# FFN up projection: high and low activation halves in one 512-column matmul, two partial sums added on VectorE

## What is computed

```python
def dwconv3(z, w, b=None):
    zp = jnp.pad(z, ((0, 0), (1, 1), (0, 0)))
    y = zp[:, :-2] * w[0] + zp[:, 1:-1] * w[1] + zp[:, 2:] * w[2]
    return y if b is None else y + b

def conv_ffn(h, w_up, conv_w, conv_b, w_down):
    gate, up = jnp.split(dwconv3(h @ w_up, conv_w, conv_b), 2, axis=-1)
    return (jax.nn.silu(gate) * up) @ w_down
```

## Time and profile before

| | us |
|---|---|
| median of three runs (2726.76 to 2734.9) | 2727.99 |
| the profiled execution, its own time | 2725.87 |
| its span, first to last instruction | 2724.2 |
| TensorE busy in the span | 2587.2 (95%) |
| VectorE / ScalarE / GpSimd busy | 1747.4 / 1118.2 / 262.9 |
| mean granted TensorE clock | 0.973 of full speed |

### The profile page before, as it was taken

One profiled execution on the slowest core, in us unless ns is written; L12 is line 12 of the kernel. 1 busy time (PEld: TensorE's weight loads), 2 busy tenths in 40 slices (PEclk: granted clock), 3 DMA queues, 4 the chain that ended last, 5 costly groups with the idle time before them and its releaser, 6 DMA issues.

```text
span 2724.2 us, 44977 instructions
## 1 busy us (share of the span) xinstructions
PE 2587.2 (95%) x16773; PEld 2350.9 (86%) x16773; DVE 1747.4 (64%) x2134; ACT 1118.2 (41%) x1377; POOL 262.9 (10%) x246
## 2 busy tenths in 40 slices
PE   4999989799999999996999999998899999999998
PEld 4989877798998988985888888886699989998997
DVE  4455455678777877667566666665556665666666
ACT  3444343443443443445233333333444434443443
POOL 2100004000000000003000000000011100110110
PEclk9999999899999999997999999998999999999999
DMA  6743369578777777872666655652545565556555
GB/s 160 240 124 95 116 191 273 197 240 277 230 246 254 252 240 244 259 241 85 212 192 191 186 183 184 189 175 96 164 129 181 184 206 172 183 179 207 174 172 172
DMA packets 277979, 523.94 MB, mean 192 GB/s; under 512 B 30696, under 2 KB 100896, under 8 KB 277088
## 3 DMA queue, kind: packets, MB, share of 16 engines
q1 hardware_dynamic: 251616, 403.66, 46.5%
q0 software_dynamic: 25536, 118.29, 14.5%
q10 hardware_dynamic: 704, 0.29, 0.0%
HBM read 511.68 MB, written 10.49 MB: 192 GB/s over the span
## 4 chain that ended last, share of the span: by engine, by line
PE 47%; DVE 3%; ACT 1%; POOL 1%; issue 1%; DMA 0%; POOLq 0%; ACTq 0%; DVEq 0%; SPq 0%
PE ps L1501 17%; PE ps L1509 11%; PE ps L1849 6%; PE ps L1860 5%; PE ps L1854 3%; PE ps L1817 1%; PE ps L1796 1%; POOL alo L533 1%; PE ps L1825 1%; DVE acc L1222 1%; DVE wlo L961 1%; PE ps L1805 1%; ACT whi L624 0%; PE ps L1751 0%; DVE arena L1445 0%
## 5 line engine op out<-in xcount | busy, mean ns | idle before, releaser
L961 DVE TENSOR_TENSOR wlo<-raw,whi 128x1024 fp32r<-128x1024 f32 (+2 forms) x776 | 989.2, 1285 | 663.3 <-ACT whi L624 640.2
L624 ACT ACTIVATE whi<-raw 128x1024 fp32r<-128x1024 f32 (+2 forms) x776 | 803.5, 1040 | 1130.2 <-PE ps L1501 462.9
L1501 PE MATMUL ps<-ahi,whi 128*128 128x256 f32 (+2 forms) x2816 | 803.9, 285 | 24.1 <-DVE wlo L961 16.6
L1501 PE MATMUL ps<-alo,whi 128*128 128x256 f32 (+2 forms) x2816 | 801.3, 285 | 0.0
L1501 PE MATMUL ps<-ahi,wlo 128*128 128x256 f32 (+2 forms) x2816 | 801.0, 284 | 0.0
L1501 PEld LDWEIGHTS ps<-ahi,whi 128*128 128x128 f32 (+1 forms) x2816 | 541.9, 192 | 28.5 <-issue 17.7
L1501 PEld LDWEIGHTS ps<-alo,whi 128*128 128x128 f32 (+1 forms) x2816 | 541.9, 192 | 0.1
L1501 PEld LDWEIGHTS ps<-ahi,wlo 128*128 128x128 f32 (+1 forms) x2816 | 541.8, 192 | 0.0
L1509 PE MATMUL ps<-whi,ahi 128*128 128x512 f32 (+2 forms) x1304 | 507.9, 390 | 18.2 <-DVE wlo L961 14.8
L1509 PE MATMUL ps<-whi,alo 128*128 128x512 f32 (+2 forms) x1304 | 502.1, 385 | 0.0
L1509 PE MATMUL ps<-wlo,ahi 128*128 128x512 f32 (+2 forms) x1304 | 501.7, 385 | 0.0
(11 more groups left out here) (253 smaller groups left out, 2345.7 us busy)
## 6 DMA issues: line engine op xcount, KB each, us to landing
arena<-in_w_ada POOLq DMA_DIRECT2D x128, 768.0 KB, 5.6
raw<-in_ffn_w_up SPq DMA_DIRECT2D x160, 512.0 KB, 4.4
raw<-in_w_mlp_in SPq DMA_DIRECT2D x128, 512.0 KB, 4.7
raw<-in_w_mlp_out SPq DMA_DIRECT2D x128, 512.0 KB, 4.8
raw<-in_na_w_qkv SPq DMA_DIRECT2D x96, 512.0 KB, 4.7
raw<-in_ffn_w_down SPq DMA_DIRECT2D x84, 512.0 KB, 4.4
raw<-in_w_in SPq DMA_DIRECT2D x64, 384.0 KB, 3.5
raw<-in_w_in SPq DMA_DIRECT2D x32, 512.0 KB, 4.5
```

The costliest lines, as they stand in the source:

```text
L624: act.activation(a, b, ACT.Copy).then_inc(hi_done, 1)
L961: dve.tensor_tensor(a, b, c, ALU.subtract).then_inc(lo_done, 1)
L1501: ins = pe.matmul(o, a, b, start=start and i == 0, stop=last and i == 2, skip_group_check=True)
```

## The change

The activations' halves become the two planes of one tensor `act2`. For each (k, chunk) step the new `unit_merged` loads the weights' high part once and streams 512 columns, the 256 high and the 256 low ones, into one bank; then the weights' low part meets the 256 high columns, added to the first half of the bank. So each chunk takes a bank of its own and a group four (`Z[q]`, all eight banks for both groups), and the result stands in two halves that have to be added. ScalarE copies the second half of each bank to a new tile `zz[q]` in SBUF (`conv_copy`), VectorE adds the first half to it (`conv_sum`), and `conv_a` and `conv_v` then read `zz[q]`. The PSUM is given back (`drained[q]`) after the sum and no longer after the taps. The down projection is unchanged but for its accumulators' banks (`GD`).

```diff
-        ahi = sb("ahi", [P, KC, 2 * S], F32R)
-        alo = sb("alo", [P, KC, 2 * S], F32R)
+        act2 = sb("act2", [P, 2, KC, 2 * S], F32R)
+        ahi, alo = act2[:, 0], act2[:, 1]
...
+        Z = [ps[:, 4 * q:4 * q + 4, :] for q in range(2)]
+        GD = [ps[:, 4 * q:4 * q + 2, :] for q in range(2)]
...
+        zz = [area(7168 + 1024 * q, 1024) for q in range(2)]
...
-            def conv_a(pair, q, nc_, used):
+            def conv_copy(pair, q, nc_, used):
 
                 act.wait_ge(unit_used, used)
+                act.activation(zz[q][:, 0:S * nc_].rearrange("p (c t) -> p c t", t=S), Z[q][:, 0:nc_, S:2 * S], ACT.Copy)                    .then_inc(z_half, 1)
+
+            def conv_a(pair, q, nc_, summed):
+
+                act.wait_ge(drained[q], summed)
                 dst = (held, cvt)[q]
                 act.wait_ge(f_h, pair * 3 + AHEAD)
                 for c in range(nc_):
                     at = C_CONV + q * FC + c
-                    ins = act.activation(dst[:, S * c:S * c + S], Gf[q][:, S * c:S * c + S], ACT.Identity,
+                    ins = act.activation(dst[:, S * c:S * c + S], zz[q][:, S * c:S * c + S], ACT.Identity,
...
-            def conv_pair(pair, u0, nc_):
+            def conv_pair(pair, u0, nc_, before):
                 for j in range(4, 20):
+                    if j % 8 == 3:
+                        conv_copy(pair, j // 8 - 1, nc_, u0 + (8 * (j // 8)))
                     split(u0, j)
                     if j == 11:
-                        conv_a(pair, 0, nc_, u0 + 8)
+                        conv_a(pair, 0, nc_, before[0] + 1)
                     if j == 19:
-                        conv_a(pair, 1, nc_, u0 + 16)
+                        conv_a(pair, 1, nc_, before[1] + 1)
...
+            def conv_sum(pair, q, nc_):
+
+                dve.wait_ge(z_half, pair * 2 + (q + 1))
+                z = zz[q][:, 0:S * nc_].rearrange("p (c t) -> p c t", t=S)
+                dve.tensor_tensor(z, z, Z[q][:, 0:nc_, 0:S], ALU.add).then_inc(drained[q], 1)
+
+            def conv_v(pair, q, nc_, summed):
 
                 dst = (held, cvt)[q]
+                dve.wait_ge(drained[q], summed)
                 dve.wait_ge(f_a, pair * 3 + (1 + 2 * q))
                 for tap in (0, 2):
                     for c in range(nc_):
-                        z = Gf[q][:, S * c:S * c + S]
+                        z = zz[q][:, S * c:S * c + S]
...
                 ins.then_inc(f_v, 1)
-                dve.wait_ge(f_v, pair * 2 + (q + 1))
-                dve.sem_inc(done, 1)
-
-            def conv_pair(pair, u0, nc_):
+
+            def conv_pair(pair, u0, nc_, before):
                 for j in range(4, 20):
+                    if j % 8 == 3:
+                        conv_sum(pair, j // 8 - 1, nc_)
+                    if j == 12:
+                        conv_v(pair, 0, nc_, before[0] + 1)
                     split(u0, j)
-                    if j == 11:
-                        conv_v(pair, 0, nc_, drained[0])
-                    if j == 19:
-                        conv_v(pair, 1, nc_, drained[1])
+                conv_v(pair, 1, nc_, before[1] + 1)
...
+            def unit_merged(u0, j, q, nc_, k0):
+
+                pe.wait_ge(lo_done, u0 + (j + 1))
+                for kk in range(2):
+                    k = k0 + kk
+                    for c in range(nc_):
+                        wh, wl = kn(whi, j)[:, kk, P * c:P * c + P], kn(wlo, j)[:, kk, P * c:P * c + P]
+                        o = Z[q][:, c, :]
+                        pe.matmul(o.rearrange("p (h t) -> p h t", h=2), wh, act2[:, :, k, 0:S], start=k == 0, stop=k == KC - 1,
+                                  skip_group_check=True)
+                        ins = pe.matmul(o[:, 0:S], wl, ahi[:, k, 0:S], start=False, stop=k == KC - 1, skip_group_check=True)
+                ins.then_inc(unit_used, 1)
+
```

More of the change, by code:

```diff
@@ L324, in program @@
         x_done, stored = sem("x_done"), sem("stored")
+        z_half = sem("z_half")
         f_a, f_v, f_h = sem("f_a"), sem("f_v"), sem("f_h")
@@ L922, in conv_a @@
                     act.activation(v, v, ACT.Silu).then_inc(f_a, 1)
-            def conv_pair(pair, u0, nc_):
+            def conv_pair(pair, u0, nc_, before):
                 for j in range(4, 20):
+                    if j % 8 == 3:
+                        conv_copy(pair, j // 8 - 1, nc_, u0 + (8 * (j // 8)))
                     split(u0, j)
                     if j == 11:
-                        conv_a(pair, 0, nc_, u0 + 8)
+                        conv_a(pair, 0, nc_, before[0] + 1)
                     if j == 19:
-                        conv_a(pair, 1, nc_, u0 + 16)
+                        conv_a(pair, 1, nc_, before[1] + 1)
             with act.Fori(0, 2) as g:
                 with act.Fori(0, 4) as n:
-                    conv_pair(g * 4 + n, g * 96 + n * 16 + U_FFN, 4)
+                    conv_pair(g * 4 + n, g * 96 + n * 16 + U_FFN, 4, [g * 6 + n + D_WO[q] for q in range(2)])
                 with act.Fori(0, 4) as n:
@@ L938, in _ @@
             with act.Fori(0, 2) as n:
-                conv_pair(n + 8, n * 16 + U_LAST, 4)
-            conv_pair(10, U_LAST + 32, 3)
+                conv_pair(n + 8, n * 16 + U_LAST, 4, [n + D_F1[q] for q in range(2)])
+            conv_pair(10, U_LAST + 32, 3, [2 + D_F1[q] for q in range(2)])
             for j in range(4, 24):
@@ L1409, in _, with add_gated @@
                 dve.tensor_tensor(alo[:, k, S:2 * S], oT[:, k, :], f(ahi[:, k, S:2 * S]), ALU.subtract).then_inc(a_lo, 1)
-            def add_gated(n, q, used, done, count, gate):
+            def add_gated(n, q, used, done, count, gate, acc=G):
                 dve.wait_ge(unit_used, used)
@@ L1416, in add_gated @@
                 tt = tmp.rearrange("p (r n) -> p r n", r=RT)
-                dve.tensor_tensor(tt, G[q], gg, ALU.mult).then_inc(done, 1)
+                dve.tensor_tensor(tt, acc[q], gg, ALU.mult).then_inc(done, 1)
                 dve.wait_ge(done, count)
@@ L1433, in _ @@
             turn(5, 0, lambda k: coefs[:, 32 + k:33 + k], lambda k: mods[:, 48 + k:49 + k])
-            def conv_v(pair, q, nc_, done):
+            def conv_sum(pair, q, nc_):
[3 more added lines that the diff above has]
+            def conv_v(pair, q, nc_, summed):
                 dst = (held, cvt)[q]
+                dve.wait_ge(drained[q], summed)
                 dve.wait_ge(f_a, pair * 3 + (1 + 2 * q))
@@ L1468, in _ @@
                             add_gated(n * 2 + q, q, g * 96 + n * 16 + (U_FFN + 64 + 8 * q + 8), drained[q],
-                                      g * 6 + n + (D_WO[q] + 4 + 1), gb2)
+                                      g * 6 + n + (D_WO[q] + 4 + 1), gb2, GD)
             with own.loop(0, 2, 2) as n:
-                conv_pair(n + 8, n * 16 + U_LAST, 4)
-            conv_pair(10, U_LAST + 32, 3)
+                conv_pair(n + 8, n * 16 + U_LAST, 4, [n + D_F1[q] for q in range(2)])
+            conv_pair(10, U_LAST + 32, 3, [2 + D_F1[q] for q in range(2)])
             for j in range(4, 24):
@@ L1476, in _ @@
                     n = j // 6 - 1
-                    add_gated(n, n % 2, U_DOWN + 6 * n + 6, drained[n % 2], D_F1[n % 2] + 3 + n // 2 + 1, gb2)
+                    add_gated(n, n % 2, U_DOWN + 6 * n + 6, drained[n % 2], D_F1[n % 2] + 3 + n // 2 + 1, gb2, GD)
                     dve.sem_inc(x_done, 1)
-            add_gated(3, 1, U_DOWN + 24, drained[1], D_F1[1] + 3 + 2, gb2)
+            add_gated(3, 1, U_DOWN + 24, drained[1], D_F1[1] + 3 + 2, gb2, GD)
             dve.sem_inc(x_done, 1)
@@ L1527, in unit_rows @@
                     for r in range(RT):
-                        ins = rows(G[q][:, r, 0:w], j, kk, 0, k, t0 + P * r, k == 0, k == final)
+                        ins = rows(acc[q][:, r, 0:w], j, kk, 0, k, t0 + P * r, k == 0, k == final)
                 ins.then_inc(unit_used, 1)
@@ L1911, in pair_units @@
                     for j in range(8):
-                        unit_columns(u0, 8 * q + j, q, nc_, 2 * j, 0)
+                        unit_merged(u0, 8 * q + j, q, nc_, 2 * j)
             with pe.Fori(0, 2) as g:
@@ L1924, in _ @@
                                 pe.wait_ge(f_h, g * 12 + (12 + AHEAD))
[L1925 removed]
+                            unit_rows(g * 96 + n * 16 + (U_FFN + 64), 8 * q + j, q, 2 * j, S, acc=GD)
             with pe.Fori(0, 2) as n:
```

5 lines of the change are left out of this document (2 added, 3 removed).

## The result

| | before | after |
|---|---|---|
| median, runs (us) | 2729.5, 11 runs (2724.07 to 2734.9) | 2741.76, 11 runs (2737.1 to 2746.26) |
| profiled execution, its span | 2725.87, 2724.2 | 2743.21, 2741.2 |
| TensorE / VectorE / ScalarE / GpSimd busy | 2587.2 / 1747.4 / 1118.2 / 262.9 | 2584.2 / 1751.8 / 1141.8 / 297.1 |

The ratio is 1.0044, 95% interval 1.0034 to 1.0054: the change makes the kernel 12 us slower. The forecast of 2723 with a range to 2732 was wrong, and wrong in its sign.

What follows compares the result with a forecast made beforehand. TensorE was taken as the bound: -18.3 us from its steps, plus stalls of 7.3, 1.7, 1.0, 1.7 and 1.7, gives -4.9, so 2721 profiled and 2723 us as median, range 2712 to 2732.

Steps and rivals of the forecast that it cites:

- TensorE as the bound: Up and down projections: TensorE never waits until 2619, so time saved on it counts in full if the others keep up.
- the count of the q=0 chain: End of a q=0 group: copy, sum, bias, taps, silu, split add 1.67 us; TensorE stalls 0.73, in ten pairs 7.3.
- VectorE's split ahead of GpSimd after q=1: End of a q=1 group: the split starts right behind the taps at 8.0, ahead of GpSimd, ends at 9.15; no stall.
- stall around the last pair: End of pair 9: 1.0 us more stall; q=0 group of the last pair: 1.7 more; together 2.7.
- GpSimd pays: product to 11.5, a split to 12.55: After a q=1 group, GpSimd and VectorE's splits alternate; GpSimd's low part ends at 16.8 us, before 14.4.
- two inner passages: Up to down projection: hidden tile at 17.0 us after the group, wanted at 16.16; stall 0.85 each, 1.7 together.
- The last passage: Last change to the down projection: hidden tile at 13.8 us, wanted at 10.7; stall 3.3, 1.7 more than before.
- the step of 0.3467: Up projection: a (k, chunk) step falls from 0.3600 to 0.3467 us; over 1376 steps 18.3 us off.
- third rival: Merged matmul reading two planes far apart regains its fixed 13 ns, steps stay at 0.360; +8 us, 2736; chance 0.08.
- The forecast's stalls: Added TensorE waits after q=0 groups 7.3 us, inner passages 1.7, pair 9 1.0, last pair 1.7, last passage 1.7.

Runs made afterwards that it cites:

- experiment 5: The changed kernel with ScalarE doing the silu after the split of unit 12 instead of before it; 2734.71 us, ratio 1.0017 to the kernel before.
- experiment 1: The changed kernel with VectorE waiting for its own q=1 taps (f_v) before it splits on; 2742.08 us, ratio 1.0040 to the kernel before.
- experiment 6: On top of experiment 5, VectorE waits for its own first split behind a q=1 group before starting the second; 2724.76 us, ratio 0.9981 to the kernel before.
- experiment 2: The changed kernel with both activation planes interleaved, so the merged matmul streams 512 contiguous columns; 2739.91 us, ratio 1.0037 to the kernel before.
- 8: The changed kernel without copy and sum, first bank halves read, and the weights' low part also streaming 512 columns; 2852.0 us in one run.

## Why the prediction was wrong

**What held.** TensorE as the bound; the count of the q=0 chain, 7.3 against 7.8 us in all, though with two errors of 0.2 each that cancel; the silu in front of the split as what makes it late (experiment 5); VectorE's split ahead of GpSimd after q=1; a bit more stall around the last pair (2.7 forecast, 1.6 found).

**The step that failed: "GpSimd pays: product to 11.5, a split to 12.55".** It let GpSimd in after one split, because before the two took turns. In the kernel after the product came 0.89 us before the second split and still waited for that and the third. The Trainium skill (SBUF — State Buffer, Who interferes with whom) says that whoever issues first gets the port for a whole instruction; the trace agrees for the product and the first split, and does not for the other two splits, which the product preceded by 0.89 and 2.02 us and still went behind. The turns of the earlier trace rows were taken by splits that GpSimd had already held up; the splits behind the taps now run unhindered, and the rule read off the one did not carry to the other. That this is what costs, two experiments show: with GpSimd first the product takes 2.42 (1), and with one wait of VectorE, a gap of 0.12 us, 3.23 and not 5.50 (6). TensorE restarted 19.2 us after the group (2189.86 - 2170.62) where the forecast said 17.0, so 2.2 later, 4.5 us in two inner passages.

**What the prediction left out: TensorE's clock after the wait.** It priced a wait at its length and nothing behind it. In the profiled execution 1.6 to 1.9 us followed at each of three passages, 5 us in all. Counted with the late tile, an inner passage is 0.85 + 2.2 + 1.6 = 4.65, measured 4.73. The last passage was forecast at 3.3; its product took 4.94 where the smaller one took 1.85 before, its low part only 1.80 where the trace before has 2.67, and with 1.9 for the clock that makes 3.3 + 3.1 - 0.9 + 1.9 = 7.4, measured 7.43. Of the 19.0 us between forecast and result, passages are 7.8 + 4.1 = 11.9.

**The term that was mis-sized: the step of 0.3467.** It is 0.3522 in the mean, 0.3533 most of the time, and that took 7.7 us of the 18.3. The unlikely third rival had named the sign (the merged matmul's bounds were "between 0.2267 and 0.240") but for the wrong reason, planes far apart; experiments 2 and 8 exclude that. At the measured step the gain is 10.6. The forecast's stalls were 13.4 at its own step and, by rival 3, some 8 at a step of 0.360; in proportion that is an estimated 11 at 0.3522. So with no other mistake the result would have been about even with the kernel before, and not 5 us faster.

**The smaller terms** around the last pair came out 1.1 us better than forecast. The sum: 7.7 + 11.9 + 0.5 (q=0) - 1.1 = 19.0, from -4.9 to +14.1.

**Still open.** Why some waits of about 3 us leave the clock at full rate and others do not; what decides between steps of 0.3467 and 0.3533; why unhindered splits keep GpSimd out where held-up ones let it in. In the fastest variant that computes everything (experiment 6) the last passage still stalls 5.81 us where it was 1.62; there copy and sum stand directly in the chain, and no shorter chain was tried.

## What to carry to other kernels

A stage that joins two matmuls pays only if what it adds afterwards stays off the chain to the next wait: here 10 us of gain met 22 of costs, and moving one silu and adding one kind of wait turned 12 us slower into 4 us faster. When VectorE and GpSimd meet on SBUF, look not only at who starts first but at whether VectorE's instructions run unhindered one behind the other, and open a gap where GpSimd's result is on the path. Where a change makes a wait of TensorE longer, expect that half clock may follow it and read the granted clock there. And a mean of distances can hide two rates: look at it stretch by stretch.

## What the runs showed of the hardware

- Unhindered VectorE splits back to back shut a waiting GpSimd instruction out: product 2.42 us when it starts first (experiment 1), 3.23 behind one split and a gap of 0.12 (6), 5.50 behind three splits (after), 6.73 behind four (after, end of pair 9). Behind a split that had been held up GpSimd got in with no gap (before, 1, 6): its low part took 3.13 to 3.17.
- A 512-column and a 256-column float32r matmul in turns take 0.3467 or 0.3533 us a pair, one rate from a wait of TensorE to the next; each kind by itself takes 0.2267 and 0.1200. The two planes of the moving operand cost nothing (experiment 2).
- After 2.87 us without a matmul TensorE was at its 1.2 GHz level, and the next eight 512-column matmuls took 0.43 each; after 3.15 us at another place, and after 2.89 us in experiment 5, it was at 2.4 GHz.
